# Attention keys and values: from TensorE transposes to 32x32 block transposes on VectorE, placed by transfers

## The reference, cut to what matters

```python
qa, ka, va, fa, qb, kb, vb = jnp.split(h @ w_in, SPLITS, axis=-1)
...
p = jax.nn.softmax(s, axis=-1).astype(v.dtype)
return jnp.einsum('nhqk,nkhd->nqhd', p, v)
...
lb = min(BAND_PAST, h.shape[1])
return y, (ka, va, logf, kb[:, -lb:], vb[:, -lb:])
```

## Time and profile before

| | us |
|---|---|
| median of 3 runs | 1230.61 |
| lowest, highest | 1228.83, 1235.47 |
| span of the profiled execution | 1226.7 |
| TensorE busy in it | 1098.9 (90%) |
| VectorE, ScalarE, GpSimd busy | 492.8, 355.7, 363.3 |
| mean granted TensorE clock | 0.958 |

### The profile page before, as it was taken

One profiled execution on the slowest core, in us unless ns is written; L12 is line 12 of the kernel. 1 busy time (PEld: TensorE's weight loads), 2 busy tenths in 40 slices (PEclk: granted clock), 3 DMA queues, 4 the chain that ended last, 5 costly groups with the idle time before them and its releaser, 6 DMA issues. The chain is left out here.

```text
span 1226.7 us, 20113 instructions
## 1 busy us (share of the span) xinstructions
PE 1098.9 (90%) x7196; PEld 769.1 (63%) x7196; DVE 492.8 (40%) x1307; ACT 355.7 (29%) x1130; POOL 363.3 (30%) x306
## 2 busy tenths in 40 slices
PE   5799999999999999999986999953999999989955
PEld 2478788888888788888865888841333333333322
DVE  0742444444444354454554277754111211111227
ACT  2841343434343333434354122110111111111102
POOL 1232524536351404022032244424222222121001
PEclk9899999999999999999998999975999999999978
DMA  9963314242230504030086422126999999989775
GB/s 381 405 216 105 113 50 132 70 123 78 75 105 16 153 1 134 1 93 25 27 240 197 164 72 75 69 96 258 383 385 374 418 413 397 410 361 420 277 288 180
DMA packets 86809, 238.63 MB, mean 195 GB/s; under 512 B 10456, under 2 KB 58024, under 8 KB 75952
## 3 DMA queue, kind: packets, MB, share of 16 engines
q1 hardware_dynamic: 68384, 132.01, 31.0%
q10 hardware_dynamic: 7344, 78.91, 15.9%
q0 software_dynamic: 10976, 26.32, 5.8%
HBM read 208.19 MB, written 38.45 MB: 201 GB/s over the span
## 5 line engine op out<-in xcount | busy, mean ns | idle before, releaser
L1968 PE MATMUL moe_gu_ps<-a_gu,moe_xT_sb 128*64 x416 | 184.8, 598 | 6.0 <-DMA b_gu<-in_w_gu 4.0
L918 PE MATMUL att_piece_ps<-hT_hi,w_hi 128*128 128x384 f32 (+1 forms) x528 | 185.2, 351 | 2.4 <-PEq L196 1.0
L1971 PE MATMUL moe_gu_ps<-b_gu,moe_xT_sb 128*64 128x512 f32 x416 | 184.9, 598 | 0.0
L918 PE MATMUL att_piece_ps<-hT_hi,w_lo 128*128 128x384 f32 (+1 forms) x528 | 173.7, 329 | 0.0
L918 PE MATMUL att_piece_ps<-hT_lo,w_hi 128*128 128x384 f32 (+1 forms) x528 | 173.3, 328 | 0.0
L1143 DVE COPY att_pT_sb<-att_pT_ps 128x512 f32<-128x512 f32 (+2 forms) x192 | 94.5, 520 | 134.9 <-PE att_pT_ps L986 134.3
L1968 PEld LDWEIGHTS moe_gu_ps<-a_gu,moe_xT_sb 128*64 128x64 f32 x416 | 57.0, 138 | 126.3 <-issue 126.3
L1248 ACT ACTIVATE att_probs_sb<-att_probs_sb,att_nmax_sb 128x640 f32<-128x640 f32 (+5 forms) x144 | 101.2, 703 | 42.9 <-DVE att_nmax_sb L1129 42.1
L1266 ACT ACTIVATE keep_rows_all_sb<-att_o_ps,att_rden_sb 128x64 f32<-128x64 f32 x144 | 37.3, 310 | 246.7 <-PE att_o_ps L1007 246.7
L918 PEld LDWEIGHTS att_piece_ps<-hT_hi,w_hi 128*128 128x128 f32 x528 | 99.8, 189 | 11.2 <-issue 6.7
L1129 DVE CUSTOM_DVE_ANT_0 att_probs_sb<-att_s_ps,both_wide_sb 128x640 f32<-128x640 f32 (+5 forms) x144 | 95.1, 661 | 27.3 <-PE att_s_ps L974 15.0
(11 more groups left out here) (312 smaller groups left out, 1958.1 us busy)
## 6 DMA issues: line engine op xcount, KB each, us to landing
b_gu<-in_w_gu ACTq DMA_DIRECT2D x25, 2048.0 KB, 17.0
b_dn<-in_w_dn ACTq DMA_DIRECT2D x25, 1024.0 KB, 10.4
keep_rows_all_sb<-in_w_ada SPq DMA_DIRECT2D x10, 2048.0 KB, 12.0
a_gu<-in_w_gu SPq DMA_DIRECT2D x10, 2048.0 KB, 13.1
att_w_raw_sb<-in_w_qkv SPq DMA_DIRECT2D x21, 512.0 KB, 3.8
a_dn<-in_w_dn SPq DMA_DIRECT2D x10, 1024.0 KB, 20.4
w_out_parts<-keep_rows_all_sb SPq DMA_DIRECT2D x16, 512.0 KB, 4.9
in_w_ada_sb<-in_w_ada SPq DMA_DIRECT2D x2, 2048.0 KB, 19.8
```

Of the source, the lines that this page charges most:

```text
L918: ins = pe.matmul(bank[:, 0:hi - lo], w[:, kind, kc, :], x[:, kc, lo:hi], start=(m == 0), stop=(m == 3 * NC - 1))
L1968: pe.matmul(gu_ps[p % 2][LANE[0], :], xT[:, c, LANE[0]], a_gu[:, bass.ds(slot, 1), c, :].rearrange("p a n -> p (a n)"), start=(c == 0), st ...
L1971: ins = pe.matmul(gu_ps[p % 2][LANE[1], :], xT[:, c, LANE[1]], b_gu[p % 3][:, c, :], start=(c == 0), stop=(c == NC - 1))
```

## The change

VectorE transposes the PSUM bank of a K or V piece in 32x32 blocks, and this takes the place of the exact copy, of TensorE's transposes and of the copies to rows. A block transpose leaves block (i, m) at its place (partitions 32i, columns 32m), so that partition 32i + a, column 32m + b holds token 32m + a, head column 32i + b. Four transfers (one for each i) write the runs of 32 values to their rows in DRAM: for K, into the outputs themselves; for V, into a new DRAM tensor `v_tokens`, from which each chunk is loaded into `v_rows`, and from there stored to the outputs as before. The values of tiles 0, 3 and 6 wait for their chunk's load (`v_ld`). SP's list is put in a new order, with the sends at their pieces. The body of the piece on VectorE and SP's functions:

```diff
-    k_rows = s.sb("k_rows", [P, TILES, P])
+    k_blocks, v_blocks = s.sb("k_blocks", [P, 3 * P]), s.sb("v_blocks", [P, 3 * P])
...
+        def store_blocks(blocks, rows, done):
+
+            for i in range(P // 32):
+                sp.dma_start(rows[:, 32 * i:32 * i + 32].rearrange("(m a) b -> a m b", a=32),
+                             blocks[32 * i:32 * i + 32, :].rearrange("a (m b) -> a m b", b=32)).then_inc(done, 16)
+
+        def store_k(n, c):
+            sp.wait_ge(piece_out, PARTS * n + PIECES.index((K, c)) + 1)
+            for lo, hi, rows in k_parts(n, c):
+                store_blocks(k_blocks[:, lo:hi], rows, k_stored)
+
+        def send_v(n, c):
+            lo, hi = CHUNKS[c]
+            sp.wait_ge(piece_out, PARTS * n + PIECES.index((V, c)) + 1)
+            store_blocks(v_blocks[:, 0:hi - lo], k["v_tok"][n, lo:hi, :], v_sent)
+
+        def load_v(n, c):
+            lo, hi = CHUNKS[c]
+            sp.wait_ge(v_sent, 64 * (3 * n + c + 1))
+            if c == 0 and n >= 2:
+                sp.wait_ge(o_ready, TILES * (n - 1))
+                sp.wait_ge(v_stored, 32 * (n - 1))
+            end = min(hi, SEQ)
+            sp.dma_start(v_rows[n % 2][:, lo // P:end // P, :], k["v_tok"][n, lo:end, :].rearrange("(t p) n -> p t n", p=P))\
+              .then_inc(v_ld[c], 16)
+            if hi > SEQ:
+                sp.dma_start(v_rows[n % 2][0:DEC, NT, :], k["v_tok"][n, SEQ:hi, :]).then_inc(v_ld[c], 16)
+
+        def store_v(n):
+            for c in range(3):
+                sp.wait_ge(v_ld[c], (16, 16, 32)[c] * (n + 1))
...
         for n in range(EARLY + 2, HALVES):
             sp.wait_ge(k["mrow_ready"], last_in_home(n) + 1)
             sp.dma_start(late_w(n), a["w_ada"][n]).then_inc(k["w_ld"][W_HOME[n]], 16)
+            if n == EARLY + 2:
+                send_v(0, 0)
+                load_v(0, 0)
...
+        store_k(0, 1)
+        send_v(0, 1)
+        load_v(0, 1)
+        store_k(0, 2)
         sp.wait_ge(k["mrow_ready"], HALVES)
         load_wo(0)
         load_w(4)
         load_w(5)
-        store(0, "k", k_rows, k_stored)
+        send_v(0, 2)
+        load_v(0, 2)
         for n in range(ALL):
-            store(n, "v", v_rows[n % 2], v_stored)
+            store_v(n)
             if n + 1 < ALL:
                 load_cache(n + 1)
                 if banded(n + 1):
                     load_rel(n + 1)
+                store_k(n + 1, 0)
+                send_v(n + 1, 0)
                 if n < PAIRS:
                     store_wo(2 * n)
+                load_v(n + 1, 0)
+                if n < PAIRS:
                     load_wo(2 * n + 1)
                 if n + 2 < ALL:
                     load_w(3 * (n + 2))
...
+                store_k(n + 1, 1)
                 if n < PAIRS:
                     store_wo(2 * n + 1)
                 if n + 1 < PAIRS:
                     load_wo(2 * n + 2)
+                send_v(n + 1, 1)
+                load_v(n + 1, 1)
+                if not banded(n + 1):
+                    load_forget(n + 1)
+                store_k(n + 1, 2)
+                if n + 2 < ALL:
+                    load_w(3 * (n + 2) + 1)
+                if not banded(n + 1):
+                    load_forget_s(n + 1)
+                send_v(n + 1, 2)
+                if n + 2 < ALL:
+                    load_w(3 * (n + 2) + 2)
+                load_v(n + 1, 2)
...
+            if at in (0, 3, 6):
+                pe.wait_ge(v_ld[at // 3], (16, 16, 32)[at // 3] * (n + 1))
...
             if kind == V:
                 dve.wait_ge(piece_ready, PARTS * n + p + 1)
-                dve.wait_ge(pT_ready, turn["rows", n, p - 1] + 1)
-                dve.tensor_copy(exact[:, 0:hi - lo], bank[:, 0:hi - lo]).then_inc(piece_out, 1)
+                dve.wait_ge(v_sent, 64 * (3 * n + c))
+                dve.transpose(v_blocks[:, 0:hi - lo], bank[:, 0:hi - lo]).then_inc(piece_out, 1)
                 return
...
+            if k_parts(n, c):
+                dve.wait_ge(k_stored, 16 * k_stores(n, c))
+                ins = dve.transpose(k_blocks[:, 0:hi - lo], bank[:, 0:hi - lo])
+            ins.then_inc(piece_out, 1)
...
-            act.activation(exact[:, 0:hi - lo], bank[:, 0:hi - lo], ACT.Copy)
```

More of the change, by code:

```diff
@@ L649, in attention @@
     pT_ready, pT_out, cache_hi = s.sem("pT_ready"), s.sem("pT_out"), s.sem("cache_hi")
-    k_stored, v_stored = s.sem("k_stored"), s.sem("v_stored")
+    k_stored, v_stored, v_sent = s.sem("k_stored"), s.sem("v_stored"), s.sem("v_sent")
+    v_ld = [s.sem(f"v_ld{c}") for c in range(3)]
     s_ready, max_done, exp_done = s.sem("s_ready"), s.sem("max_done"), s.sem("exp_done")
@@ L669, in after, with k_parts, k_stores @@
         return (n, at) if at < TILES else (n + 1, 0)
-    def rows_piece(n, at):
-        n, p = (n + 1, at - 1) if at else (n, PARTS - 1)
-        return (n, p) if n < ALL and PIECES[p][0] != Q else None
-    turn, turns = {}, 0
[L677 to L683, removed]
+    def k_parts(n, c):
+        lo, hi = CHUNKS[c]
+        letter = "b" if banded(n) else "a"
+        prompt, sample = o[f"k_{letter}_prompt"], o[f"k_{letter}_sample"]
+        first = SEQ - prompt.shape[0]
+        begin, end = max(lo, first), min(hi, SEQ)
+        cols = slice(n % PAIRS * P, n % PAIRS * P + P)
+        parts = [(begin - lo, end - lo, prompt[begin - first:end - first, cols])] if begin < end else []
+        return parts + ([(SEQ - lo, TOK - lo, sample[:, cols])] if hi > SEQ else [])
+    def k_stores(n, c):
+        return sum(4 * len(k_parts(m, d)) for m in range(ALL) for d in range(3) if (m, d) < (n, c))
+    turn, turns = {}, 0
+    turn["logf"] = turns
+    turns += 1
     turn["cache", 0] = turns
@@ L768, in in_columns @@
+        def store_v(n):
+            for c in range(3):
+                sp.wait_ge(v_ld[c], (16, 16, 32)[c] * (n + 1))
+            t0 = NT - o["v_b_prompt"].shape[0] // P if banded(n) else 0
+            dst = o[f"v_{group(n)}_prompt"][:, columns(n)]
+            sp.dma_start(dst.rearrange("(t p) n -> p t n", p=P), v_rows[n % 2][:, t0:NT, :]).then_inc(v_stored, 16)
+            sp.dma_start(o[f"v_{group(n)}_sample"][:, columns(n)], v_rows[n % 2][0:DEC, NT, :]).then_inc(v_stored, 16)
         def in_columns(rows):
@@ L811, in _ @@
                     load_w(3 * (n + 2))
[L812 to L816, removed]
                 if n == 0:
@@ L922, in project @@
                 ins.then_inc(piece_ready, 1)
[L924 to L931, removed]
-                r = rows_of(3 * c + m)
-                ins = pe.transpose(pT_ps[e % 2][0:r, m, :], exact[:, m * P:m * P + r], ident)
-            ins.then_inc(pT_ready, 1)
         def cache_columns(n):
@@ L950, in scores @@
             t, r, kb, wide, _ = tile(n, at)
-            pe.wait_ge(piece_out, PARTS * n + needs(at))
+            pe.wait_ge(piece_out, PARTS * n + needs(at) if n or at else PARTS - 1)
             if t == NT:
@@ L1031, in _ @@
             project(0, p)
-            if p and PIECES[p - 1][0] != Q:
-                to_rows(0, p - 1)
             if p == LOGF_AT:
@@ L1173, in _ @@
             piece(0, p)
-            if p and PIECES[p - 1][0] != Q:
-                rows_out(0, p - 1)
             if p == 1:
@@ L1230, in piece @@
                 return
-            if n or p:
-                act.wait_ge(pT_ready, turn["rows", *((n, p - 2) if p else (n - 1, PARTS - 2))] + 1)
-            act.activation(exact[:, 0:hi - lo], bank[:, 0:hi - lo], ACT.Copy)
             if c < 2:
```

51 lines of the change are left out of this document (10 added, 41 removed).

## The result

| | before | after |
|---|---|---|
| median, us | 1229.72 (4 runs) | 1203.32 (4 runs) |
| lowest, highest, us | 1228.82, 1235.47 | 1200.73, 1205.21 |
| ratio, 95% interval | | 0.977 [0.974, 0.979] |
| span of the profiled execution, us | 1226.7 | 1198.9 |

The change makes the kernel 2.3% faster; the forecast was 1209.3 us, 1.7%, with a range from 1197 to 1236. The profiled execution itself took 1200.73 us, 1.8 more than its span; the forecast had added 3.9 us for this, the distance of the median to another run's span.

The account below looks back on a forecast made before the run. TensorE's instruction list was taken to bound the attention stage. Terms -29.8 + 7 + 1 + 0.5 = -21.3 us took the span from 1226.7 to 1205.4; 3.9 added gave 1209.3 us, range 1197 to 1236.

Parts of the forecast that it names:

- new cache waits with their half clocks: TensorE's waits for `cache_k`: 7 us in pair 0, half clock included, and 1 us over banded pairs 1 to 3.
- TensorE, removed: Attention: 48 `to_rows` groups at 0.32 us (15.4), waits of 13.9 and small start gains go; 29.8 us saved.
- Rival (d): The 13.9 us of waits come back at cache transposes or values: about 1223 us, chance counted inside (b).
- Six groups of the prologue: `to_rows` groups before 125 us, removed at 0.32 us each; the prologue ends about 2 us earlier.
- VectorE, ScalarE: About 41.6 us of copies removed, 44 block transposes at 0.55 us (24 us) added; slack makes this worth nothing.
- The K chain's charge: K's PSUM bank is freed 0.1 us later, after its transpose: 0.5 us charged, 3 us at the high bound.
- DMA: 208 block transfers, 61,440 descriptors of 128 bytes at 20 ns (between 7 and 29): 77 us beside TensorE's work.
- SP's queue in pair 0: A 14 us chain from `send_v(0, 2)` lands `cache_k` near 142 us, wanted at 137: 5 us wait, 2 us half clock.
- Banded pairs 1 to 3: The chain from V's last chunk to `cache_k` ends about when TensorE needs it: a tie, 1 us for three.
- Forgetting pairs: Cache issued 3 us later costs nothing, being wanted well after; pair 4 keeps its existing 2.2 us wait.
- (b): Sends dearer by S us a chunk: S = 3 gives 1217 to 1224 us (0.14), S = 5 1224 to 1237 (0.14).
- (c): Cache wait in every pair makes the kernel slower, from S = 6 us more a chunk; 1264 us at S = 10; chance 0.15.

Follow-up runs that it names:

- e10: The kernel after, unchanged, run and profiled again: 1201.37 us, ratio 0.976 to the kernel before.
- e9: The kernel before, with `to_rows` behind the second half projection and `cache_k` loaded on its own ahead of `load_w(3(n + 2) + 2)`: 1207.41 us, ratio 0.980.
- e2: The kernel after, with 42 groups of three unit-matrix transposes, which wait for nothing, given back to TensorE: 1211.50 us, ratio 0.984.
- e6: The kernel after, with `cache_k` loaded ahead of `send_v(n, 2)`, and `send_v(n, 1)` and `load_v(n, 1)` ahead of the `w_out` round trip: 1186.91 us, ratio 0.964.
- e1: The kernel before, with only `to_rows` moved behind the second half projection and every transpose kept: 1210.01 us, ratio 0.982.
- e8: The kernel after, with each pair's last V chunk sent four times, three of them into DRAM that nothing reads: 1221.86 us, ratio 0.993.
- e3: The kernel after, with the `cache_k` load parted from `cache_v` and issued ahead of `send_v(n, 2)`: 1193.70 us, ratio 0.969.
- e4: The kernel after, with each of VectorE's 44 block transposes made twice: 1203.03 us, ratio 0.976.
- e11: The kernel after, with `cache_k` and `send_v(n, 1)`/`load_v(n, 1)` moved early, and `load_w(3(n + 2) + 2)` behind `load_v(n + 1, 2)`: 1186.07 us, ratio 0.966.
- e5: The kernel after, with each pair's last V chunk sent twice, once into DRAM that nothing reads: 1201.61 us, ratio 0.976.
- e7: The kernel after, with `load_w(3(n + 2) + 2)` moved behind `load_v(n + 1, 2)`: 1192.96 us, ratio 0.970.

## Why the prediction was right, point by point

The account of the stretch, from pairs of kernels. With e10's stretch in place of after's the last two rows would be +11.2 and -24.0:

| | predicted, us | measured, us | from |
|---|---|---|---|
| stalls at the banks `pT_ps` | -13.9 | -21.1 | before to e9, less the cache's 3.9 |
| instructions, 42 groups | -13.4 | -14.1 (e2: 12.2 or 8.6) | e9 to e6 |
| new cache waits with their half clocks | +8 | +7.6 | after to e6 (11.5), less the 3.9 of before |
| sum | -19.3 | -27.6 | 499.7 - 527.3 |

- **TensorE, removed: right, and one term too small.** The spacing of 0.32 us was right, and the duration would have been wrong by a factor of two. The term for the waits was taken as the profile prints them, and it left out the six waits before `cache_columns`, which go too: 21.1 instead of 13.9 us, of which the 21 stalls before `to_rows` cost 17.6. This is the largest error, and most of the 6 us by which the forecast was too high. Rival (d), by which the waits would come back elsewhere, is excluded by e1. The 0.5 us by which TensorE's start wait of 1.7 us was to shrink didn't come: it is 1.7 us in after as well.
- **Six groups of the prologue: right in size, not seen in the result.** From the first matmul of the first piece to the first cache transpose, 50.2 us passed before and 50.2 in e1, without a half clock; 48.1 and 48.2 in e8 and e3, again without one. That is 2.1 us (1.9 predicted, 6 x 0.32). In the profiled execution of after it was 49.7, since the clock stood at 0.50 for about 3.4 us at its start:

```profile
76.00:78.00 2.00, 2.00 (x9) 2.00 (x8) 0.00 (x0) 0.00 (x0) 0.00 (x0) 0.55 0.68 189
```

Such a stretch near 76 us stands in 8 of 10 traces of kernels with blocks and in one of three without (e9, 51.7 us). Too few to say whether the change has a part in it; what differs wasn't tried.
- **VectorE, ScalarE: right.** 0.55 us for a block transpose, no price by itself. The K chain's charge of 0.5 us was generous (0.3 us of waits, 0.8 before); e4 doubles the transpose, which is the high bound of 1.1 us: 6.2 us of waits, where the bound charged 3.
- **DMA: right, cheaper than taken.** 13 ns a packet in the bracket of 7 to 29. In the stretch of e6 nothing waits for these transfers.
- **SP's queue in pair 0: the right place, too large.** `send_v(0, 2)` was issued at 130.1 and TensorE had its cache at 141.2, 11.1 us later; 14 were predicted. So the chain started 2 us later than forecast and ran 3 us shorter, and the cache was there at 141.2 where 142 was forecast. The wait was still 1.2 us, not 5, and the larger part of that is that TensorE came to it at 140.0 us and not at 137. Its clock was at 0.50 for about 3.4 us longer at two places ahead of it, near 76 us and here, from 128 to over 134 us, where before it rose after 131:

```profile
132.00:134.00 2.00, 2.00 (x8) 1.90 (x8) 0.56 (x4) 0.00 (x0) 0.94 (x1) 0.50 0.74 160
```

The forecast had a half clock behind the cache wait; this one stands ahead of it, and isn't its price. In e6 and e11, which have no cache wait in pair 0, the clock is as long at 0.50 there, and in e2, which has one of 1.4 us, it is not. What makes it longer in most kernels with blocks isn't shown.
- **Banded pairs 1 to 3: the step that failed.** The prediction led the chain from the sends and called it a tie for 1 us in three pairs. The waits were 0, 2.0 and 0.8 us, with one half clock; e5 shows that the sends of the last chunk were not on the chain, and e7 that it ran through the weight load that I had listed among the things "moved past" and costed at nothing. I had looked at whom that load makes late on TensorE, not at what SP holds back behind it. The timelines (e5) carry it one link further back, to K's eight issues of 4 us ahead of the weight load before, which the prediction had put at "so nothing" by the same argument.
- **Forgetting pairs: pairs 5 and 6 free as predicted; pair 4** waited 4.2 us instead of keeping its 2.2.
- All new waits and clocks together were charged at 8 us. In the stretch they were 7.6 (11.2 in e10). That the sum fits is partly luck: pair 0 was overcharged (7 us against 1.2, or 2.9 with the longer half clock ahead of it), pairs 2 to 4 undercharged.
- **The rivals.** (b) and (c) needed dear sends; they cost 13 ns a packet. The point from which (c) decides was set at 6 us more in each pair. e8 put 6 us of issues there and came out 8.8 us faster than the kernel before, 20 us slower than after where the rival's formula gives 4 x 6 + 3 x 1 = 27: the formula lacked the slack at `load_w`. Its waits were 0.6 to 8.4 us from pair to pair, so no one slope describes them.

Behind these rows: a transfer of less than 512 bytes was to cost a read, a modification and a write by the Trainium skill ("DMA: Bandwidth & Descriptors", Specifications). The trace shows 13 ns for 128 bytes into DRAM, beside 29 ns for packets of nearly all 512 bytes: less for a packet, 1.8 times as much for a byte. Whether such a price is part of the 13 ns no run here separates.

## What to carry to other kernels

A printed wait of TensorE ahead of short instructions can be less than it costs: these stalls of 0.66 us cost 0.84 each. Moving the stalled instructions behind work that needs nothing gave 22 of the 26 us without any new mechanism, so try the order first. On an engine that issues transfers in one written order, find what it stands at just ahead of the transfer that is late; the chain runs through the last such wait, so ask in turn what that one waited for. A transfer put past it (one load here, 9 us) can be worth more than a cheaper transfer. Profile the same kernel twice before reading 4 us out of one trace. After each mending read the waits again: the cache wait hid a late send worth another 5 us.

## What the runs showed of the hardware that was not expected

- A printed wait of 0.72 us ahead of short transposes costs TensorE 0.92 us (1.53 us for the step instead of 0.61), since the transposes would otherwise start 0.11 us apart though each has a duration of 0.27.
- 128-byte runs into DRAM cost 13 ns a packet and land in 1.9 us for 48 KB (median of 64), no slower than a 64 KB load of the cache (2.1 to 2.7 us, after). Eight transfers in a row instead of four (e5) landed in time all the same.
- VectorE transposes a 128x384 float32 PSUM tile in 32x32 blocks in 0.57 to 0.58 us (after, this width alone), about as long as the plain copy of it took (0.56 us).
- After a wait of 4.2 us the clock stood at 0.5 (1.2 GHz) for the 3.5 us that followed, and was at 1.00 from 407.4 to 410 us:

```profile
403.90:407.40 3.50, 3.50 (x12) 3.20 (x11) 0.36 (x2) 0.75 (x5) 3.42 (x2) 0.52 0.18 28
```

So this wait cost 1.7 us more than it shows. The wait of 2.0 us at 269 us was followed by as long a half clock, and behind one of 4.6 us in e10 the clock stayed at 0.50 for another 5 us. After the wait of 0.8 us at 335 us, nothing of the kind is in the trace.
